# Inverting the chunks' triangular matrices in two diagonal blocks of 64, side by side

## The reference

```python
decay = jnp.exp(jnp.where(incl, gc[..., :, None] - gc[..., None, :], -jnp.inf))
lower = jnp.where(strict, jnp.einsum('bhncd,bhnsd->bhncs', kb, k) * decay, 0.0)
a_mat = lower + jnp.eye(chunk, dtype=lower.dtype)
rhs = jnp.concatenate([vb, kb * jnp.exp(gc)[..., None]], axis=-1)
sol = lax.linalg.triangular_solve(a_mat, rhs, left_side=True, lower=True, unit_diagonal=True)
u, w = sol[..., :DV], sol[..., DV:]
```

## Time and profile before

| | us |
|---|---|
| median of 3 runs | 2262.46 |
| the profiled execution, whole | 2264.14 |
| its span, first to last instruction | 2262.5 |
| `stage_chunks` in it, 609.05 to 846.20 | 237.15 |
| busy: PE, PEld | 1989.5, 1667.1 |
| busy: DVE, ACT, POOL | 1209.3, 681.1, 314.2 |

### The profile page before, as it was taken

How to read it: one execution, slowest core, us unless ns; L and a number is a source line. 1 busy time by engine, 2 the same in 40 slices (tenths; PEclk the granted TensorE clock), 3 DMA queues, 4 the chain that set the end, 5 groups by cost and what they waited for, 6 DMA issues and landing times. The chain is left out here.

```text
span 2262.5 us, 31252 instructions
## 1 busy us (share of the span) xinstructions
PE 1989.5 (88%) x11652; PEld 1667.1 (74%) x11652; DVE 1209.3 (53%) x2239; ACT 681.1 (30%) x1331; POOL 314.2 (14%) x360
## 2 busy tenths in 40 slices
PE   5998999954688986589899869799999999999998
PEld 5877799954388876356654438688899888899886
DVE  3264677995465546666433235644444444444446
ACT  4332267745511110055332114421211211211213
POOL 4323324534211100000113310000000000000000
PEclk9998999986799989689999979999999999999999
DMA  4323322110100001150388844121111111111102
GB/s 139 83 67 100 89 85 57 38 28 0 48 1 1 1 1 38 57 209 1 118 283 313 294 167 161 54 86 38 38 39 46 65 38 38 38 40 45 65 29 79
DMA packets 144418, 176.41 MB, mean 78 GB/s; under 512 B 29080, under 2 KB 99865, under 8 KB 144140
## 3 DMA queue, kind: packets, MB, share of 16 engines
q1 hardware_dynamic: 130220, 131.94, 18.6%
q0 software_dynamic: 14048, 42.48, 5.7%
HBM read 155.86 MB, written 18.01 MB: 77 GB/s over the span
## 5 line engine op out<-in xcount | busy, mean ns | idle before, releaser
L2345 PE MATMUL banks<-front_h_hi,front_w_hi 128*128 128x364 f32 (+2 forms) x744 | 257.9, 347 | 52.8 <-ACT work L852 26.0
L2345 PE MATMUL banks<-h_hi,ml_up_hi 128*128 128x364 f32 (+1 forms) x768 | 253.0, 329 | 10.0 <-DVE ml_up_lo L2681 10.0
L2346 PE MATMUL banks<-h_lo,ml_up_hi 128*128 128x364 f32 (+1 forms) x768 | 252.8, 329 | 0.0
L2347 PE MATMUL banks<-h_hi,ml_up_lo 128*128 128x364 f32 (+1 forms) x768 | 252.8, 329 | 0.0
L2346 PE MATMUL banks<-front_h_lo,front_w_hi 128*128 128x364 f32 (+2 forms) x744 | 250.5, 337 | 0.0
L2347 PE MATMUL banks<-front_h_hi,front_w_lo 128*128 128x364 f32 (+2 forms) x744 | 250.2, 336 | 0.0
L2720 DVE TENSOR_TENSOR x<-x,banks 128x512 f32<-128x512 f32 x256 | 175.8, 687 | 125.6 <-PE banks L2347 125.3
L2345 PE MATMUL banks<-ml_down_hi,ml_hid_hi 128*128 128x512 f32 (+1 forms) x576 | 224.5, 390 | 2.5 <-DVE ml_hid_lo L2700 2.5
L2346 PE MATMUL banks<-ml_down_lo,ml_hid_hi 128*128 128x512 f32 (+1 forms) x576 | 224.4, 390 | 0.0
L2347 PE MATMUL banks<-ml_down_hi,ml_hid_lo 128*128 128x512 f32 (+1 forms) x576 | 224.1, 389 | 0.0
L2345 PEld LDWEIGHTS banks<-front_h_hi,front_w_hi 128*128 128x128 f32 (+1 forms) x744 | 144.0, 194 | 69.2 <-POOL front_w_lo L644 26.4
(11 more groups left out here) (407 smaller groups left out, 3494.0 us busy)
## 6 DMA issues: line engine op xcount, KB each, us to landing
upper<-in_cache_k SPq DMA_DIRECT2D x128, 256.0 KB, 4.3
upper<-in_cache_v POOLq DMA_DIRECT2D x112, 256.0 KB, 4.6
arena<-in_w_up SPq DMA_DIRECT2D x32, 512.0 KB, 4.3
arena<-in_w_down SPq DMA_DIRECT2D x32, 512.0 KB, 5.9
work<-in_w_in SPq DMA_DIRECT2D x30, 512.0 KB, 3.9
op_raw<-in_w_out SPq DMA_DIRECT2D x24, 512.0 KB, 3.5
arena<-in_x_prompt SPq DMA_DIRECT2D x8, 512.0 KB, 5.6
upper<-in_cache_v SPq DMA_DIRECT2D x16, 256.0 KB, 3.9
```

The source lines that it names most:

```text
L2345: pe.matmul(out, lh, rh, start=start, stop=False)
L2346: pe.matmul(out, lh, rl, start=False, stop=False)
L2347: return pe.matmul(out, ll, rh, start=False, stop=stop)
```

## The change

The inverse of a 128x128 lower triangular matrix is built from its two diagonal blocks of 64 and one cross block. `ZM` and `X` become 64 columns wide per head: partitions 0 to 63 hold the upper diagonal block and partitions 64 to 127 the lower one. Each product is issued per head for both blocks. The block on partitions 0 to 63 reads rows 0 to 63 and writes columns 0 to 63 of the array, the other reads rows 64 to 127 and writes columns 64 to 127; both results go to the same PSUM bank, on different partitions. Levels 1 to 5 run in this form. The last level is replaced by two products for the cross block, 64x64 each per head: `Lm`'s cross block times the lower inverse, negated by ACT on its way into `X`, then the upper inverse times that, copied by ACT into `full`, the assembled 128x128 inverse which the solve reads. The lower left corner of `full` is set to zero once. The level masks shrink to 64 columns, and the constants by 512 columns. POOL's first operation becomes two of 64 partitions for a prompt chunk. The wait for POOL moves from the X product of level 1 to its Y products. The sample chunk keeps its three levels on 64 rows.

```diff
--- before.py
+++ after.py
...
 S_LEVELS = 3
...
+    half, hcol = row % HALF, np.arange(HALF)[None, :]
+    for l in range(LEVELS - 1):
         s = 1 << l
-        lev.append(-1.0 * ((row // (2 * s) == col // (2 * s)) & (row // s % 2 == 0) & (col // s % 2 == 1)))
+        lev.append(-1.0 * ((half // (2 * s) == hcol // (2 * s)) & (half // s % 2 == 0) & (hcol // s % 2 == 1)))
     parts["level"] = np.concatenate(lev, 1)
-    parts["first_low"] = -1.0 * ((row // 2 == col // 2) & (row % 2 == 1) & (col % 2 == 0))
+    parts["first_low"] = -1.0 * ((half // 2 == hcol // 2) & (half % 2 == 1) & (hcol % 2 == 0))
+    parts["ident_half"] = half == hcol
     parts["score_causal"] = NEG_SCORE * (col > row)
     parts["score_new"] = NEG_SCORE * ~(s_ok & (col <= row))[:, :NS]
     parts["attn_causal"] = MASKED * (col > row)
@@ -113,7 +116,7 @@
     return np.ascontiguousarray(np.concatenate([np.asarray(parts[n], np.float32) for n in names], 1)), where
 
...
-LASTING = 12053
+LASTING = 12053 - 256
...
-    kbe, vb, Lm, X, TG = ([k.view(m.take(512), G, P) for m in t_at] for _ in range(5))
-    ZM = [k.view(m.take(1024), 2 * G, P) for m in t_at]
+    kbe, vb, Lm, TG, full = ([k.view(m.take(512), G, P) for m in t_at] for _ in range(5))
+    ZM = [k.view(m.take(512), 2 * G, HALF) for m in t_at]
+    X = [k.view(m.take(256), G, HALF) for m in t_at]
...
+    IN_HALF = LEVELS - 1
+    levels = lambda t: IN_HALF if t < NT else S_LEVELS
+    halves = lambda t: [(slice(i * HALF, (i + 1) * HALF), slice(i * HALF, (i + 1) * HALF)) for i in range(2 if t < NT else 1)]
...
+    def half_bank(s, i):
+        return k.psum[4 * s + i].rearrange("p (h n) -> p h n", n=HALF)
...
-                for l in range(steps):
+                for l in range(IN_HALF):
-                        r = rows_of(t)
                         if l == 0:
                             pe.wait_ge(built[s], i + 1)
                         else:
-                            if l == 1:
-                                pe.wait_ge(low_made[s], 2 * i + 2)
-                            pe.wait_ge(grown[s], LEVELS * i + l)
+                            pe.wait_ge(grown[s], IN_HALF * i + l)
                         for h in range(G):
-                            if l == 0:
-                                last = pe.transpose(bank(s, 2, r)[:, h, :], Lm[s][0:r, h, 0:r], k.c["ident"][0:r, 0:r])
-                            else:
-                                last = pe.matmul(bank(s, 2, r)[:, h, :], Lm[s][0:r, h, 0:r], ZM[s][0:r, h, 0:r], start=True, stop=True)
+                            for rows, cols in halves(t):
+                                right = ZM[s][rows, h, :] if l else k.c["ident"][rows, cols]
+                                last = pe.matmul(half_bank(s, 2)[rows, h, :], Lm[s][rows, h, cols], right, start=True, stop=True)
                         last.then_inc(x_made[s], 1)
                     for s, t in enumerate(pair):
                         if l >= levels(t) or l == 0:
                             continue
-                        r = rows_of(t)
-                        pe.wait_ge(masked[s], (LEVELS - 1) * i + l)
+                        if l == 1:
+                            pe.wait_ge(low_made[s], 3 * i + len(halves(t)) + 1)
+                        pe.wait_ge(masked[s], (IN_HALF - 1) * i + l)
                         for h in range(G):
-                            last = pe.matmul(bank(s, 0, r)[:, h, :], ZM[s][0:r, G + h, 0:r], X[s][0:r, h, 0:r], start=True, stop=True)
-                        if l < levels(t) - 1:
-                            for h in range(G):
-                                last = pe.matmul(bank(s, 1, r)[:, h, :], X[s][0:r, h, 0:r], ZM[s][0:r, G + h, 0:r], start=True, stop=True)
+                            for rows, cols in halves(t):
+                                last = pe.matmul(half_bank(s, 0)[rows, h, :], ZM[s][rows, G + h, :], X[s][rows, h, :], start=True, stop=True)
+                        for h in range(G):
+                            for rows, cols in halves(t)[0:2 if l < levels(t) - 1 else 1 if t < NT else 0]:
+                                last = pe.matmul(half_bank(s, 0)[rows, G + h, :], X[s][rows, h, :], ZM[s][rows, G + h, :], start=True, stop=True)
+                        last.then_inc(y_made[s], 1)
+                a, b = slice(0, HALF), slice(HALF, P)
+                for s, t in enumerate(pair):
+                    if t < NT:
+                        pe.wait_ge(lower[s], i + 1)
+                        for h in range(G):
+                            last = pe.matmul(half_bank(s, 2)[a, h, :], Lm[s][b, h, a], full[s][b, h, b], start=True, stop=True)
+                        last.then_inc(x_made[s], 1)
+                for s, t in enumerate(pair):
+                    if t < NT:
+                        pe.wait_ge(grown[s], IN_HALF * (i + 1))
+                        pe.wait_ge(crossed[s], 2 * i + 1)
+                        for h in range(G):
+                            last = pe.matmul(half_bank(s, 0)[a, h, :], ZM[s][a, G + h, :], X[s][a, h, :], start=True, stop=True)
                         last.then_inc(y_made[s], 1)
                 for s, t in enumerate(pair):
                     r = rows_of(t)
-                    pe.wait_ge(grown[s], LEVELS * i + levels(t))
+                    if i == 0:
+                        pe.wait_ge(cleared, S)
+                    if t < NT:
+                        pe.wait_ge(crossed[s], 2 * i + 2)
+                    else:
+                        pe.wait_ge(grown[s], IN_HALF * i + levels(t))
                     for h in range(G):
-                        pe.matmul(k.psum[4 * s + 2][0:r, h * P:(h + 1) * P], ZM[s][0:r, h, 0:r], vb[s][0:r, h, :], start=True, stop=True)
+                        pe.matmul(k.psum[4 * s + 2][0:r, h * P:(h + 1) * P], full[s][0:r, h, 0:r], vb[s][0:r, h, :], start=True, stop=True)
                     for h in range(G):
-                        last = pe.matmul(k.psum[4 * s + 3][:, h * P:h * P + r], kbe[s][0:r, h, :], ZM[s][0:r, h, 0:r], start=True, stop=True)
+                        last = pe.matmul(k.psum[4 * s + 3][:, h * P:h * P + r], kbe[s][0:r, h, :], full[s][0:r, h, 0:r], start=True, stop=True)
                     last.then_inc(solved[s], 1)
...
+                a, b = slice(0, HALF), slice(HALF, P)
+                for s, t in enumerate(pair):
+                    if t < NT:
+                        act.wait_ge(x_made[s], LEVELS * (i + 1))
+                        act.activation(X[s][a], half_bank(s, 2)[a, 0:G, :], ACT.Copy, scale=-1.0).then_inc(crossed[s], 1)
+                for s, t in enumerate(pair):
+                    if t < NT:
+                        act.wait_ge(y_made[s], IN_HALF * (i + 1))
+                        act.copy(full[s][a, :, b], half_bank(s, 0)[a, 0:G, :]).then_inc(crossed[s], 1)
...
-                    ident, low = (c[0:r, 0:r].unsqueeze(1).to_broadcast([r, G, r]) for c in (k.c["ident"], k.b["first_low"]))
+                    ident, low = (k.b[n][0:r, :] for n in ("ident_half", "first_low"))
+                    wide = lambda x, n: x.unsqueeze(1).to_broadcast([n, G, HALF])
                     pool.wait_ge(built[s], i + 1)
-                    pool.tensor_tensor(TG[s][0:r, :, 0:r], Lm[s][0:r, :, 0:r], low, ALU.mult).then_inc(low_made[s], 1)
-                    pool.wait_ge(low_made[s], 2 * i + 1)
+                    if s:
+                        pool.wait_ge(low_made[0], 3 * i + 3)
+                    elif i:
+                        pool.wait_ge(low_made[1], 3 * i)
+                    for half, (rows, cols) in enumerate(halves(t)):
+                        pool.tensor_tensor(TG[s][rows, :, 0:HALF], Lm[s][rows, :, cols], wide(low[rows], HALF), ALU.mult).then_inc(low_made[s], 1)
+                        pool.wait_ge(low_made[s], 3 * i + half + 1)
                     if i:
                         pool.wait_ge(solved[s], i)
-                    pool.tensor_tensor(ZM[s][0:r, G:2 * G, 0:r], TG[s][0:r, :, 0:r], ident, ALU.add).then_inc(low_made[s], 1)
+                    pool.tensor_tensor(ZM[s][0:r, G:2 * G, :], TG[s][0:r, :, 0:HALF], wide(ident, r), ALU.add).then_inc(low_made[s], 1)
...
+            for s in range(S):
+                dve.memset(full[s][HALF:P, :, 0:HALF], 0.0).then_inc(cleared, 1)
...
-                for l in range(steps):
+                for l in range(IN_HALF):
...
+                        mask = k.b["level"][0:r, l * HALF:(l + 1) * HALF].unsqueeze(1).to_broadcast([r, G, HALF])
                         dve.wait_ge(x_made[s], LEVELS * i + l + 1)
-                        if l == 0:
-                            ident = k.c["ident"][0:r, 0:r].unsqueeze(1).to_broadcast([r, G, r])
-                            up = k.b["level"][0:r, 0:r].unsqueeze(1).to_broadcast([r, G, r])
-                            dve.tensor_tensor(X[s][0:r, :, 0:r], bank(s, 2, r), up, ALU.mult).then_inc(first[s], 1)
+                        last = dve.tensor_tensor(X[s][0:r], half_bank(s, 2)[0:r, 0:G, :], mask, ALU.mult)
```

(54 more changed lines are left out.)

## The result

The changed kernel takes 2192.68 us, the median of four runs (2192.12 to 2194.83), against 2263.44 for the kernel before on the same chip: a ratio of 0.969, 95% interval 0.967 to 0.971. The forecast was 2203, with a range of 2190 to 2240. The profiled execution took 2192.8 us with a span of 2191.2, 71.3 less than before.

The account below looks back on a forecast made before the run. PE, in a loop with DVE's add, was taken to bound a level. Per pair 0.3 + 3.5 + 7.4 + 4.6 = 15.8, four pairs 63, less 4 for the clock: 59 off 2264.1, 2205, or 2203 by median; range 2190 to 2240.

Parts of the forecast that it names:

- level 0: First level of a pair: only DVE's mask and identity add shorten, saving 0.3 us, bounds -0.1 and 0.6.
- level 1: Second level of a pair: POOL's operations become hidden and it takes 3.7 us instead of 7.17, saving 3.5.
- three levels: From the start of level 2 to that of level 5: each takes 3.56 us instead of 6.04, saving 7.4 per pair.
- level 5 to the solve: End of a pair, with the cross block's two products: 5.8 us instead of 10.45, saving 4.6, bounds 3.5 and 5.3.
- x: Time a group of eight 64x64 products, 16 records, holds PE: 0.50 us, bounds 0.44 to 0.61.
- the loop's rest: Part of a level outside its five PE groups, DVE's add with hand-overs: falls from 1.59 to 1.06 us.
- The clock: TensorE's falls to 1.2 GHz in three of four pairs stay; longer or new falls cost 1 us per pair.
- The first rival: In the levels, corners take turns at full clock, a group taking 0.89 us: 2235 us in all, chance 0.11.
- The second rival: In the levels, corners take turns at 1.2 GHz, a group taking 1.78 us: about 2305 us, chance 0.10.
- The third: Corners run together, but the levels of every pair stay at 1.2 GHz: 2255 us, chance 0.07.

Follow-up runs that it names:

- sets 1 and 2: Changed kernel with unused 64x64 products added in the second pair, two opposite corners alternating, into one bank or two: 0.93 us each for 32 records.
- set 8: Changed kernel with unused 64x64 products added in the second pair, using all four corners: each corner starts a record every 0.06 us.
- one-corner kernel: Changed kernel with levels 1 to 5 making the upper block's products twice and leaving out the lower block's: 2251.01 us, 0.990 of before.
- set 4: Changed kernel with unused 64x64 products added in the second pair, all in one corner: 1.81 us for 32 records.
- set 3: Changed kernel with unused 64x64 products added in the second pair, eight of one corner and then eight of the other: 1.46 us.
- the order within a group: Changed kernel with each group's four upper-block products issued first, then the four lower, instead of in turn: 2204.27 us, 0.974 of before.
- the kernel with POOL's wait: Changed kernel with the wait for POOL put back ahead of level 1's X product instead of the Y products: 2200.33 us, 0.972 of before.

## Why the prediction was right

The mechanism was the one forecast, corners that run together at mostly full clock, and the time fell 10 us below the forecast. That it stayed inside the range is in part luck: it lies 2.7 us above the lower end, and the second measurement of the same kernel, 2188.95, lies below it. By the forecast's own terms, per pair at full clock:

| step | before | forecast | measured | saved: forecast | measured |
|---|---|---|---|---|---|
| level 0 | 2.98 | 2.7 | 2.24 | 0.3 | 0.7 |
| level 1 | 7.17 | 3.7 | 3.29 | 3.5 | 3.9 |
| three levels | 18.1 | 10.7 | 10.0 | 7.4 | 8.1 |
| level 5 to the solve | 10.45 | 5.8 | 6.11 | 4.6 | 4.3 |
| sum | | | | 15.8 | 17.0 |

- **The group of products.** x is 0.47, near the lower bound of 0.44 and not the 0.61 of the earlier trace rows. With the loop's rest at 1.0 (1.06 forecast) that makes the level 3.33. Taking 0.50 and 1.06 cost 0.7 us over three levels.
- **Level 0** saved 0.7, outside its bounds (-0.1 to 0.6): both of DVE's operations came to 0.42 from 0.68 and 0.71, which is 0.55. The other 0.2 lies in hand-overs that the step left out: DVE's next operation starts 0.11 behind the X group's start for 0.20, and the X product of level 1 starts 0.06 behind the add for 0.14. Why is not shown.
- **Level 1**: POOL is hidden, as forecast, but with little to spare: its last operation ends at 661.73 and the Y group of stream 1 starts at 661.95.
- **The end** is 0.3 longer than forecast. The step placed the wait rightly (stream 1's lower add), and had it end at 4.1 where it ends at 677.16 - 672.92 = 4.2. From there it let ACT's copy of stream 0 bring the solve. That copy is done at 678.58; what PE's order still puts ahead of the solve is the second cross product of stream 1, which waits for ACT's negation, starts at 678.45 and is followed by the solve at 679.03.
- **The clock** is the step that failed, by sign. It kept today's three falls and added 1 us a pair. Beyond four undisturbed pairs, the kernel before lost 217.6 - 4 x 51.94 = 9.9 us, the one after 144.4 - 4 x 35.04 = 4.2, the half-clock start of the first pair in both: a gain of 5.7, not a loss of 4. The sentence that the thin stretch "stays, thin as it was" was the error. PE was busy for 1.68 of the 3.40 us before the fall; in the same place it is now busy for 2.32, since DVE's shorter operations bring the groups closer together, and no pair fell there in two profiles of the changed kernel. The wait for POOL, moved behind the Y products, came after the falls of the kernel before and cannot have started them. What decides a fall stays open: the third pair before had the same 1.68 and did not fall, and the third pair with one corner fell with 2.52 in that place (714.00 to 717.40). New falls came in the solve, behind the thin stretch ahead of it, as feared, but few (one pair in this profile, two in the second) and at 1.6 us each, not up to 3.5.

So 59 became 71.3: 4.6 from the sum of the steps over four pairs, 9.7 from the clock, less the 1.9 given back elsewhere.

The first rival fell with sets 1 and 2. The Trainium skill's rule behind it ("TensorEngine Tiling (Array Packing)", Restrictions and Gotchas), that different row tiles cannot access one bank at the same time, does not agree with these runs where the two tiles write to different halves of the partitions: 0.93 us with one bank and with two. Both tiles on the same half of one bank were not tried. In the Trainium skill, the Tile-to-Partition Mapping of that page lists four 64x64 tiles, one for each pair of a half read and a half written, and set 8 has products run in all four at once. Turns are worth what that rival said: one corner at full clock comes to some 2230, its forecast was 2235. The second rival, turns at half clock, was met in one pair of the one-corner kernel with a group of 1.71 (forecast 1.78) and a loss of 69.46 - 51.94 = 17.5 (forecast 16). The third did not occur: the levels stay at 2.4 GHz.

## What to carry to other kernels

Block-diagonal products of half size gain on PE where neighbouring products sit in different corners; issue them in turn, one of each block, and price a pair at what one product costs. When operations shrink and waits move, work out again how thin PE's stretches get, and do not carry today's falls of the clock over: here the clock was 9.7 us of the miss and all steps together 4.6. Once products are cheap, the loop is the hand-over to the engine that updates; split the update so that the part the next product needs comes first.

## What the runs showed of the hardware

- In one corner a product is no cheaper by its column than on the whole array (set 4: 0.057 us a record of 64 columns, for 0.111 of 128), and four corners in turn share the time of one (set 8: four records in 0.06 us).
- PE starts the next corner's records about 0.17 us before the last corner is through (set 3, and the order within a group). Products of the lower rows even began ahead of earlier-issued ones of the upper rows (676.12 for line 1590, 676.23 for line 1589). That each engine executes in the order written therefore does not hold for the starts of PE's records.
- At 1.2 GHz, PE without a pause in one corner did not get its clock back in 47.8 us (third pair); in the second and fourth pair of that kernel the same work ran at 2.4 GHz throughout. In the changed kernel both corners in turn held 2.4 GHz, and in the kernel with POOL's wait such work had the clock back at 666.8, behind the fall at 663.4.
